# Rotary halves: a permutation product gives way to copies and partition-offset products

## The reference, cut to what matters

```python
def apply_rope(t, cos, sin):
    t1, t2 = jnp.split(tf, 2, axis=-1)          # halves of a head's 64 features
    return concat([t1 * c - t2 * s, t2 * c + t1 * s])

qa, ka, va, qb, kb, vb, qc, kc, vc, qi, ki, wi, ga, gb, gc = split(x @ w_in)
# rope on qi, ki (indexer), qc, kc (top-k attention), qb, kb (band), qa, ka (dilated)
```

## Time and profile before

| | |
|---|---|
| median of 3 runs | 2712.69 us (2711.89 to 2713.6) |
| profiled execution, its own time | 2713.97 us |
| its span, first to last instruction | 2712.2 us |
| PE busy | 2504.5 us (92%) |
| DVE / ACT / POOL busy | 1291.7 / 866.9 / 294.3 us |
| mean granted TensorE clock | 0.982 of full speed |
| ropes of layer 0 of the hybrid | 1532 to 1713 us of the span |
| ropes of layer 1 | 2224 to 2405 us |

### The profile page before, as it was taken

One profiled execution on the slowest core, in us unless ns is written; L12 is line 12 of the kernel. 1 busy time (PEld: TensorE's weight loads), 2 busy tenths in 40 slices (PEclk: granted clock), 3 DMA queues, 4 the chain that ended last, 5 costly groups with the idle time before them and its releaser, 6 DMA issues.

```text
span 2712.2 us, 39463 instructions
## 1 busy us (share of the span) xinstructions
PE 2504.5 (92%) x16084; PEld 1855.5 (68%) x16085; DVE 1291.7 (48%) x2254; ACT 866.9 (32%) x1474; POOL 294.3 (11%) x376
## 2 busy tenths in 40 slices
PE   7999899988898988998899999989999999989998
PEld 4664433443784433343699888879989988888997
DVE  6563323222664323221554675565455467555545
ACT  3241111110342111110344444444444444444443
POOL 0210100000000010000000212320010011233001
PEclk9989999999998999999899999999999999999999
DMA  9987999999774999999755444335646544334372
GB/s 390 343 323 320 420 419 418 412 420 418 242 280 198 420 420 419 414 420 420 278 200 185 143 125 136 124 124 198 197 155 202 187 137 156 119 116 154 132 240 79
DMA packets 253288, 712.09 MB, mean 263 GB/s; under 512 B 14514, under 2 KB 171954, under 8 KB 196786
## 3 DMA queue, kind: packets, MB, share of 16 engines
q1 hardware_dynamic: 249474, 704.94, 68.9%
q10 hardware_dynamic: 2208, 2.60, 0.3%
q0 software_dynamic: 1424, 1.98, 0.2%
HBM read 705.52 MB, written 1.05 MB: 261 GB/s over the span
## 4 chain that ended last, share of the span: by engine, by line
PE 62%; DMA 22%; issue 6%; DVE 5%; POOL 2%; ACT 2%; SPq 1%; ACTq 0%; DVEq 0%; POOLq 0%
DMA ring<-in_e_w_up_dram 19%; PE w L869 17%; PE w L1131 11%; PE y L909 9%; PE w L871 9%; DMA ring<-in_ada_w_dram 3%; PE w L1150 2%; PE w L1417 2%; PE y L776 1%; PE y L1183 1%; DVE wsp L1526 1%; POOL arena L2820 1%; PE w L1402 1%; PE w L971 1%; ACT wsp L1516 1%
## 5 line engine op out<-in xcount | busy, mean ns | idle before, releaser
L1526 DVE TENSOR_TENSOR wsp<-ring,wsp 128x1024 fp32r<-128x1024 f32 x470 | 578.8, 1237 | 400.8 <-ACT wsp L1516 400.3
L869 PE MATMUL w<-hh,wsp 128*128 128x256 f32 (+1 forms) x4800 | 634.0, 285 | 1.0 <-DVE wsp L1526 0.6
L869 PEld LDWEIGHTS w<-hh,wsp 128*128 128x128 f32 (+1 forms) x4800 | 602.8, 191 | 24.4 <-issue 11.9
L1516 ACT CAST wsp<-ring 128x1024 fp32r<-128x1024 f32 x470 | 487.9, 1045 | 389.1 <-PE w L871 208.5
L1131 PE MATMUL w<-ring,arena 128*64 128x512 f32 x2016 | 461.4, 600 | 85.1 <-DMA ring<-in_e_w_up_dram 80.1
L1131 PEld LDWEIGHTS w<-ring,arena 128*64 128x64 f32 x2016 | 154.9, 137 | 353.0 <-issue 351.2
L871 PE MATMUL w<-hl,wsp 128*128 128x256 f32 (+1 forms) x2400 | 336.6, 283 | 0.0
L871 PEld LDWEIGHTS w<-hl,wsp 128*128 128x128 f32 (+1 forms) x2400 | 309.5, 192 | 0.0
L909 PE MATMUL y<-wsp,zsp 128*128 128x512 f32 x1104 | 267.0, 391 | 4.1 <-DVE wsp L1526 3.8
L2012 DVE TENSOR_TENSOR ht<-w,ht 128x256 f32<-128x256 f32 x64 | 39.5, 617 | 450.9 <-ACT ht L2549 450.9
L2549 ACT ACTIVATE ht<-w 128x256 f32<-128x256 f32 x64 | 40.0, 625 | 635.7 <-PE w L1131 635.7
(11 more groups left out here) (345 smaller groups left out, 2522.6 us busy)
## 6 DMA issues: line engine op xcount, KB each, us to landing
ring<-in_e_w_gate_dram SPq DMA_DIRECT2D x126, 1024.0 KB, 8.6
ring<-in_e_w_up_dram SPq DMA_DIRECT2D x126, 1024.0 KB, 10.8
ring<-in_e_w_down_dram SPq DMA_DIRECT2D x124, 1024.0 KB, 12.0
ring<-in_ffn_in_dram SPq DMA_DIRECT2D x88, 1024.0 KB, 5.4
ring<-in_w_in_dram SPq DMA_DIRECT2D x50, 1024.0 KB, 5.2
ring<-in_ada_w_dram SPq DMA_DIRECT2D x48, 1024.0 KB, 12.2
ring<-in_ffn_out_dram SPq DMA_DIRECT2D x44, 1024.0 KB, 5.1
ring<-in_b_w_in_dram SPq DMA_DIRECT2D x12, 1024.0 KB, 10.1
```

Of the source, the lines that this page charges most:

```text
L869: pe.matmul(dst, a[:, kc * m:(kc + 1) * m], hh[:, kc, :], start=kc == 0 and j == 0, stop=False)
L1516: ac.copy(shaped(halves(i)[0], u.shape), u.cut(ring[:, u.piece % NSLOT, :])).then_inc(*mark("w_high", i))
L1526: ve.tensor_tensor(shaped(lo, u.shape), u.cut(ring[:, u.piece % NSLOT, :]), shaped(hi, u.shape).bitcast(F32), ALU.subtract).then_inc(*mark ...
```

## The change

The permutation matrix leaves the constants (128 columns fewer), the PE product leaves the rope steps, and with it the bank WB[2] as a station of the rope. The sine table is now made in four pieces of 32 partitions whose signs are +, -, -, + (`sin` is made by ACT at the start). For partitions 0 to 63 DVE reads `raw` and `sin` at the other half's 32 partitions and writes the product to its own place (two instructions). For partitions 64 to 127 ACT copies the two halves crosswise into `swap`, and DVE multiplies `swap` by `sin` in one instruction. The add and POOL's product stay.

```diff
@@ PE, step "rope": removed
-                    elif s[0] == "rope":
-                        r = ropes.index(s[1])
-                        pe.wait_ge(*at("roped_raw", key, s[1]))
-                        if second[0] is not None:
-                            pe.wait_ge(*at(*second[0]))
-                        second[0] = "roped_sin", key, s[1]
-                        pe.matmul(WB[2][:, 0:T], perm, raw[:, r % 2, :], start=True, stop=True).then_inc(*mark("turned_half", key, s[1]))
@@ DVE, step "rope"
-                        ve.wait_ge(*at("turned_half", key, s[1]))
-                        ve.tensor_tensor(dst, WB[2][:, 0:T], sin[:, :], ALU.mult).then_inc(*mark("roped_sin", key, s[1]))
+                        ve.wait_ge(*at("roped_raw", key, s[1]))
+                        for q in range(2):
+                            here, there = slice(32 * q, 32 * q + 32), slice(32 - 32 * q, 64 - 32 * q)
+                            ve.tensor_tensor(dst[here, :], raw[there, r % 2, :], sin[there, :], ALU.mult).then_inc(
+                                *mark("roped_sin", key, s[1], q))
+                        ve.wait_ge(*at("swapped", key, s[1]))
+                        ve.tensor_tensor(dst[64:128, :], swap[64:128, r % 2, :], sin[64:128, :], ALU.mult).then_inc(
+                            *mark("roped_sin", key, s[1]))
                         ve.wait_ge(*at("roped_sin", key, s[1]))
                         ve.wait_ge(*at("roped_cos", key, s[1]))
                         ve.tensor_tensor(dst, dst, rot[:, r % 2, :], ALU.add).then_inc(*mark("roped", key, s[1]))
@@ ACT, step "rope"
-                            ac.wait_ge(*at("turned_half", key, ropes[r - 2]))
+                            ac.wait_ge(*at("roped_sin", key, ropes[r - 2]))
                         ac.activation(raw[:, r % 2, :], WB[projs.index(step) % 2][:, 0:T], ACT.Copy,
                                       scale=0.125 if name in ("qc", "qb", "qa") else 1.0).then_inc(*mark("roped_raw", key, s[1]))
+                        ac.wait_ge(*at("roped_raw", key, s[1]))
+                        for q in range(2, 4):
+                            here, there = slice(32 * q, 32 * q + 32), slice(32 * (5 - q), 32 * (6 - q))
+                            ins = ac.copy(swap[here, r % 2, :], raw[there, r % 2, :])
+                        ins.then_inc(*mark("swapped", key, s[1]))
@@ ACT, start
-            ac.activation(sin[:, :], red, ACT.Sin).then_inc(*mark("sines", 0))
+            for q, sign in enumerate((1.0, -1.0, -1.0, 1.0)):
+                ins = ac.activation(sin[32 * q:32 * q + 32, :], red[32 * q:32 * q + 32, :], ACT.Sin, scale=sign)
+            ins.then_inc(*mark("sines", 0))
```

More of the change, by code:

```diff
@@ L36 @@
 ADA_AT = (0, 2, 4, 6, 8, 10, 12, 14, 16)
-C_ID, C_INV, C_SAME, C_PERM, C_MA, C_MB, C_MC, C_IO, C_IG, C_TRI, C_I5 = 0, 128, 129, 161, 289, 673, 1057, 1441, 1473, 1505, 1633
+C_ID, C_INV, C_SAME, C_MA, C_MB, C_MC, C_IO, C_IG, C_TRI, C_I5 = 0, 128, 129, 161, 545, 929, 1313, 1345, 1377, 1505
 NFIRST = 161
-NCONST = 2145
+NCONST = 2017
 CAP = 64
@@ L67, in constants @@
     c[:, C_ID:C_ID + P] = np.eye(P)
[L68 to L72, removed]
     t = np.arange(T)[:, None]
@@ L267, in program @@
         ident = const[:, C_ID:C_ID + P]
-        perm = const[:, C_PERM:C_PERM + P]
         tri = const[:, C_TRI:C_TRI + P]
@@ L329, in program @@
         dg = ht[:, 0, :, 0:P]
+        swap = ht[:, 1, :, :]
         bias_rows = ht[:, 0:2, :, :].rearrange("p a b t -> p (a b t)")
@@ L1450, in hybrid @@
                             else:
-                                pe.wait_ge(*at(*second[0]))
+                                if second[0] is not None:
+                                    pe.wait_ge(*at(*second[0]))
                                 second[0] = "p_copied", key, br, j, 1
```

## The result

| | before | after |
|---|---|---|
| median of 5 runs each | 2712.58 us | 2726.55 us (2724.32 to 2727.2) |
| profiled execution / its span | 2713.97 / 2712.2 us | 2726.55 / 2724.8 us |
| mean granted TensorE clock | 0.982 | 0.973 |

The ratio is 1.0053, with a 95% interval of 1.004 to 1.0067: 14 us slower where +6.0 was forecast. 2726.55 lies just inside the range (2701 to 2727), above the forecast's own range of 0 to +11 us, and at the time of the rival with more falls and dearer ports (2726). The range holds it by 0.45 us, and only with the part that was added for that rival: that it holds is luck.

What follows compares the result with a forecast made beforehand. PE was busy 2504.5 of 2712.2 us, but DVE would run full in the first stretch. Layer 0 +3.3 and layer 1 +2.7 made +6.0 us, 2718.7 from the median; range 2701 to 2727.

Steps and rivals of the forecast that it cites:

- rival with more falls and dearer ports: Two half-clock windows at each wait and 0.9 us for some cosine products: +13 us, 2726; chance 0.12.
- the first stretch: First nine ropes and index steps of a layer: DVE's queue fills, first index sum and PE 2.6 us late.
- port wait: Where DVE has no idle time, each POOL cosine product takes 0.45 us from it; bounds nothing or 0.9.
- the three places named: PE's small waits become long ones: about 4.4 us ahead of qc0, 5.5 ahead of kb0, 6 ahead of va0.
- The ropes qb and kb: 0.9 us lost at kb0, then 2.6 and 0.4 us come back by kb1's rope: gain 2.1 us.
- The copies are hidden: ACT's two copies take 0.75 us per rope, beside DVE's first two products, and cost nothing.
- the start: Table making before the layers: cosine table up to 1.3 us later, hidden behind a weight wait; together nothing.
- The clock: Half clock behind the long waits: 1.7 us at each of two later waits, 1.3 ahead of qc0, 4.7 per layer.
- The ropes qa and ka: PE can start va0 at about 1711.1 instead of 1712.96 us: gain 1.9 us.
- today's fall in layer 1: At the ropes qb and kb in layer 1 a clock fall exists already; 0.6 us credited for it.
- No port waits: POOL's products take nothing from DVE, the clock falls once per layer: 10 us faster, 2702.7; chance 0.18.
- The clock holds: No clock falls behind the waits: altogether 3.4 us faster, 2709.3; chance 0.25.

Runs made afterwards that it cites:

- d3: Kernel after the change with ACT's two crosswise copies 1 column wide instead of 256, half of the sine part left out: 2727.15 us, 1.005 of the kernel before.
- a1: Kernel after the change with POOL's cosine product cut to one column and the add reading the cosine table in its place: 2708.22 us, 0.9982 of the kernel before.
- a2: Kernel after the change with ACT making all four crosswise copies and DVE one sine product over 128 partitions: 2708.23 us, 0.9984 of the kernel before.
- a4_fill_wide: Kernel after the change with unread PE products of 256 columns added in PE's waits: 2716.81 us, 1.001 of the kernel before.

## Why it came out so

**Right.** PE's waits only move: the product and its stops went, and PE is idle for 12.1 and 13.5 us more per layer. DVE's queue is the bound of the first stretch: three products at 0.42, a port wait of 0.42 us where a pair meets POOL's product, the copy for wi at 23.7 us after the layer's start (forecast 23.0). The long waits came at the three places named, within 0.4 us. The ropes qb and kb came out as forecast in layer 0: -2.1 us without the clock, and kb0 18.8 us behind c0 (forecast 18.9). In the sum there is some luck, since a misreading (below) took 0.35 us off the loss at kb0, and as much more came back behind it. The copies are hidden (d3), and the start shows nothing. Neither the ports nor the added products are the cause alone: a1 takes away the first, a2 the second, and each by itself gives back all of the loss (19 us).

**The clock, the term that was most mis-sized.** The prediction bounded it by "none, or two windows at each wait". I took one of 1.7 us behind each of the two later waits and one of 1.3 behind the first, six in the two layers and 9.4 us in all. Measured: most waits are followed by 6.8 us at half clock, two windows and not one. A further fall comes behind a wait at the index steps that I had not priced, and DVE waits in turn for the slowed projections. Together there are sixteen windows of 3.4 us at half clock. Against that, a full one costs 1.4 us rather than 1.7, and PE is idle in a part of some. The sum is at least 11.6 us, by a4_fill_wide, and about 15 by the estimate there; that 9.4 came near the lower bound is errors that partly cancel. Over half of it lies in the first stretch (3.7 and 2.4 us instead of 1.3).

**The first stretch.** From DVE's first rope to the first index sum a4 takes 31.8 and 31.9 us, against 28.3 before: 3.5 us late without the clock, where 2.6 was forecast. The copy for wi has 0.2 of the difference (14.4 us behind the first rope, forecast 14.2), the way from there to the sums 0.7. Some 0.5 of that is that a rope's first product is held too: it starts 1.25 us behind a low part (1540.71 to 1541.96 above), not 1.14, and a rope takes 1.69 us, not 1.64. From the layer's start it is 3.9 and 3.4 us, since the first rope starts 0.5 us later than before in layer 0 and 0.2 sooner in layer 1. The table's +4.7 and +4.0 also hold 1.2 and 1.1 us that the fillers of a4 take among the index products; they are not the change's.

**The ropes qa and ka.** "Gain 1.9 us" was forecast, and "the softmax of b3 comes some 0.9 us later". Measured from b1: a gain of 1.0 us in both layers, with no fall on the way, and the softmax 1.1 us later (38.3 us behind b1 instead of 37.3). DVE's timeline ahead of that softmax, after and then before:

```profile
1704.21 1.22 DVE L1517 TENSOR_TENSOR wsp<-ring,wsp 128x1024 fp32r<-128x1024 f32 x1
1705.46 0.86 DVE L2165 TENSOR_TENSOR arena<-arena,sin 32x256 f32<-32x256 f32 x2
...
1707.27 0.86 DVE L2165 TENSOR_TENSOR arena<-arena,sin 32x256 f32<-32x256 f32 x2
...
1708.96 1.22 DVE L1517 TENSOR_TENSOR wsp<-ring,wsp 128x1024 fp32r<-128x1024 f32 x1
1710.10 0.28 DVE L2279 CUSTOM_DVE_ANT_0 arena<-y,const 128x128 f32<-128x128 f32 x1
```
```profile
1703.27 1.22 DVE L1526 TENSOR_TENSOR wsp<-ring,wsp 128x1024 fp32r<-128x1024 f32 x1
1704.41 0.28 DVE L2282 CUSTOM_DVE_ANT_0 arena<-y,const 128x128 f32<-128x128 f32 x1
```

So the mechanism was right. PE, without its stops, has b3's scores sooner (31.3 us behind b1 instead of 35.2), and then stands. DVE's softmax starts 6.1 us behind their end at 1703.98; before the change it started 1.1 us behind (1703.30 to 1704.41), because two ropes of 1.8 us and a low part stand ahead of it. What PE gains at its ropes it waits out ahead of va0. Of the missing 0.9 us per layer, 0.2 are the softmax, 0.3 the chain from it to va0 (6.1 us instead of the forecast's 5.8), and 0.35 a misreading of mine. I took va0 and kb0 to start, before the change, at 1712.96 and 1613.61, the end of the rope product ahead of them. But its records overlap with what follows, and they start at 1712.61 and 1613.26. In a1 and a2, which give DVE its time back, b1 to va0 takes 42.8 and 42.7 us, against 45.5 before.

**The other sizes.** The 0.6 us credited for today's fall in layer 1 was 0.1 (c0 to b1 takes 71.6 us with it and 71.5 in layer 0 without). Behind va0 there are 1.3 and 0.7 us for which I had nothing; the 1.3 has a fall of a4 in it, worth 1.4. The error in the two layers is 10 us (16.0 against 6.0). By the table 2.2 of it are the clock and 7.8 the other terms: 3.5 the first stretch, 0.4 the ropes qb and kb, 1.9 the ropes qa and ka, 2.0 behind va0. With what a4's fillers and its last fall cost put to the clock, which is an estimate, the clock has nearly 6 of the 10. The 3.4 us by which the rest of the span is shorter make the error of the whole look like 6.6 (12.6 against 6.0).

**The rivals.** "No port waits" is refuted by a1: without them the kernel is 19 us faster, and its waits and falls are fewer. "The clock holds" describes a4, which came out 3 us slower than before and not 3.4 faster, for the terms above and for what its fillers cost. "More falls, dearer ports" gave the right time and half the reason: the falls are longer, as it said, but the ports aren't dearer per product.

## What to carry to other kernels

Taking a step from the busiest engine pays only if the engine that gets it is not the one the busiest waits for next: count the work of that engine's queue between the two points where the busy one needs it, in every stretch anew. Splitting an elementwise instruction by partitions multiplied its cost here, so give such copies to the engine with room (here ACT, four copies and one product over all partitions), and look at what a second SBUF input meets on POOL. Where many short waits of PE would become a few long ones, price the half clock behind them, and try products nobody reads in the gap. And when you compare two traces stage by stage, set the borders where the terms of your forecast begin and end: one in the middle of a group of ropes puts a gain into one stage and the wait that eats it into the next.

## What the runs showed of the hardware

- A wait of PE of 2.8 to 5.6 us was mostly followed by 6.8 us at the 1.2 GHz level, in some places by 3.4; 18 matmuls of 256 columns fit into 3.4 us there instead of 31. Equal waits of 3.00 us in one execution were once followed by none and once by 6.8 us (a1).
- Fillers in a wait of PE kept the clock up: ahead of qc0 36 products of 256 columns left no fall behind them, 36 of 128 columns, with 0.82 us of idle time behind them instead of 0.49, one of 3.4 us.
- DVE instructions over 32, 64 and 128 partitions of 256 columns take 0.415, 0.423 and 0.426 us; starting in another group of partitions than the one ahead costs about 0.11 us of overlap each.
- ACT's copy of 32 partitions by 256 columns from one group of partitions to another takes 0.40 us.
- A DVE pair that reads two SBUF tensors took 1.28 us beside a product of POOL that reads SBUF and 0.86 without it; over a layer that is 0.40 and 0.33 us of DVE per product of POOL. POOL's own median rises from 738 to 910 ns.
